# Who adds up the squares of a norm, and where three small steps stand in their queues: a two-layer diffusion backbone on one core

## The reference

```python
x += 1/2 * gate1 * RMSNorm_post(SwiGLU_1(RMSNorm_pre(x) * (1 + scale1) + shift1))
x +=       gate2 * RMSNorm_post(Mixer_l (RMSNorm_pre(x) * (1 + scale2) + shift2))
x += 1/2 * gate3 * RMSNorm_post(SwiGLU_2(RMSNorm_pre(x) * (1 + scale3) + shift3))

def rmsnorm(x, g):
    xf = x.astype(jnp.float32)
    return (xf * lax.rsqrt(jnp.mean(xf * xf, axis=-1, keepdims=True) + EPS) * g).astype(x.dtype)
```

## Time and profile before

| | |
|---|---|
| median of 3 runs | 3075.51 us (3073.78 to 3078.9) |
| profiled execution | 3073.78 us, span 3072.0 us |
| mean granted TensorE clock | 0.976 |
| PE busy | 2852.7 us (93%) |
| DVE, ACT, POOL busy | 1816.0 (59%), 1040.4 (34%), 330.8 (11%) us |
| chain that ended last | PE 77%, DVE 11%, ACT 4%, POOL 3%, issue 3%, DMA 2% |
| costliest line | L1577, PE, 70% of the chain |

### The profile page before, as it was taken

How to read it: one execution, slowest core, us unless ns; L and a number is a source line. 1 busy time by engine, 2 the same in 40 slices (tenths; PEclk the granted TensorE clock), 3 DMA queues, 4 the chain that set the end, 5 groups by cost and what they waited for, 6 DMA issues and landing times.

```text
span 3072.0 us, 47247 instructions
## 1 busy us (share of the span) xinstructions
PE 2852.7 (93%) x19418; PEld 2728.2 (89%) x19418; DVE 1816.0 (59%) x2715; ACT 1040.4 (34%) x1684; POOL 330.8 (11%) x269
## 2 busy tenths in 40 slices
PE   0999999997789999999999999999878898999998
PEld 0999999986579999999999999999844598999997
DVE  7566665755657555657664646457777737532334
ACT  2311114444765211134311125653323424311123
POOL 2000002100021000012000002100027612000002
PEclk9999999999999999999999999999989998999999
DMA  5445544421033443443443433622210133422233
GB/s 190 136 151 173 162 152 139 132 90 44 22 97 116 157 151 126 151 148 107 158 153 126 154 110 119 178 87 71 90 45 28 39 103 103 124 85 68 76 98 115
DMA packets 105174, 351.36 MB, mean 114 GB/s; under 512 B 11008, under 2 KB 27648, under 8 KB 104576
## 3 DMA queue, kind: packets, MB, share of 16 engines
q1 hardware_dynamic: 99328, 339.30, 34.7%
q10 hardware_dynamic: 5632, 9.05, 0.8%
HBM read 337.69 MB, written 10.62 MB: 113 GB/s over the span
## 4 chain that ended last, share of the span: by engine, by line
PE 77%; DVE 11%; ACT 4%; POOL 3%; issue 3%; DMA 2%; DVEq 0%; ACTq 0%; POOLq 0%; SPq 0%
PE P L1577 70%; DVE cv L1467 3%; POOL nbuf L604 2%; DVE wl L1017 1%; ACT pb L807 1%; DVE st L1147 1%; PE P L1499 1%; ACT wh L696 1%; PE P L1745 1%; DMA raw<-wgu_d 1%; PE P L1816 1%; DMA mraw<-wmod_d 1%; POOL mraw L623 1%; PE P L1601 1%; PE P L1518 1%
## 5 line engine op out<-in xcount | busy, mean ns | idle before, releaser
L1577 PE MATMUL P<-xh,wh 128*128 128x320 f32 x4016 | 1021.9, 314 | 5.9 <-DVE xl L1359 4.2
L1577 PE MATMUL P<-xl,wh 128*128 128x320 f32 x4016 | 1010.1, 311 | 0.0
L1577 PE MATMUL P<-xh,wl 128*128 128x320 f32 x4016 | 1009.9, 311 | 0.0
L696 ACT CAST wh<-raw 128x1024 fp32r<-128x1024 f32 (+1 forms) x431 | 481.8, 1118 | 1031.8 <-PE P L1577 840.1
L1017 DVE TENSOR_TENSOR wl<-raw,wh 128x1024 fp32r<-128x1024 f32 (+1 forms) x431 | 574.3, 1333 | 318.5 <-ACT wh L696 318.2
L1577 PEld LDWEIGHTS P<-xh,wh 128*128 128x128 f32 x4016 | 700.5, 189 | 16.0 <-issue 12.5
L1577 PEld LDWEIGHTS P<-xl,wh 128*128 128x128 f32 x4016 | 700.1, 189 | 1.7 <-issue 1.2
L1577 PEld LDWEIGHTS P<-xh,wl 128*128 128x128 f32 x4016 | 699.9, 189 | 0.0
L604 POOL TENSOR_TENSOR nbuf<-nbuf 128x320 f32<-128x320 f32 x144 | 196.4, 1367 | 2340.7 <-ACT nbuf L711 2334.9
L1577 PE MATMUL P<-hh,wh 128*128 128x320 f32 x1408 | 383.5, 313 | 0.0
L1577 PE MATMUL P<-hh,wl 128*128 128x320 f32 x1408 | 380.5, 311 | 0.0
(11 more groups left out here) (228 smaller groups left out, 2400.0 us busy)
## 6 DMA issues: line engine op xcount, KB each, us to landing
raw<-wgu_d SPq DMA_DIRECT2D x216, 512.0 KB, 3.8
mraw<-wmod_d SPq DMA_DIRECT2D x144, 512.0 KB, 3.6
raw<-wdB_d SPq DMA_DIRECT2D x64, 704.0 KB, 4.1
raw<-wdA_d SPq DMA_DIRECT2D x32, 704.0 KB, 5.5
raw<-ain_d SPq DMA_DIRECT2D x28, 512.0 KB, 3.5
raw<-sz_d SPq DMA_DIRECT2D x26, 512.0 KB, 3.9
raw<-sx_d SPq DMA_DIRECT2D x24, 512.0 KB, 3.6
raw<-aout_d SPq DMA_DIRECT2D x16, 512.0 KB, 3.6
```

The lines of the kernel that those rows point to most:

```text
L696: nc.scalar.copy(wh[:, u.u % SPLITS, 0:n], raw[:, u.u % 2, 0:n]).then_inc(hi_done, 1)
L1577: ins = nc.tensor.matmul(P[:, u.banks[i], 0:C], w[:, u.u % SPLITS, k * 128:(k + 1) * 128], m[:, k, C * h:C * h + C], start=(k == 0 and w i ...
```

## The change

Four things, all in the order or the division of work:

1. For PRE norms POOL adds k = 2, 4 and 6 only, and PE takes 1, 3, 5 and 7. Both tables of places change, and the counters with them.
2. `dg` gets three full blocks of 128: DVE writes them with one instruction; PE spreads with two matmuls, of 256 and 64 columns.
3. On DVE, `low` of unit u+2 stands ahead of the windows' work.
4. On ACT, `decays(n)` stands behind the output step of its unit szB n.

```diff
-        ADDED = {PRE: (1, 2, 3, 4, 5, 6), POST: (1, 2, 3, 4, 5, 6)}
-        DIRECT = {PRE: (7,), POST: (7,)}
+        ADDED = {PRE: (2, 4, 6), POST: (1, 2, 3, 4, 5, 6)}
+        DIRECT = {PRE: (1, 3, 5, 7), POST: (7,)}
...
-        PRE_DIRECT = {0: {(3, 9): 7}, 1: {(6, 0): 7}}
+        PRE_DIRECT = {0: {(2, 9): 1, (3, 0): 3, (3, 6): 5, (3, 9): 7}, 1: {(3, 4): 1, (4, 4): 3, (5, 4): 5, (6, 0): 7}}
...
                 elif p.name in ("sz", "szB"):
-                    if p.name == "szB":
-                        decays(u.n)
                     i, n = z_units.index(u), p.w0 + u.n
...
                     act.dma_start(d["zspill"][n][:, c0:c1], zb[:, i % 4, c0:c1]).then_inc(z_out[i % 4], 16)
+                if p.name == "szB":
+                    decays(u.n)
...
-                V.tensor_tensor(dg[:, h, 0:256].rearrange("p (b c) -> p b c", b=2), bc_mid(ident, 2), bc_last(r3[:, h, 1, 0:2], 128), ALU.mult)
-                V.tensor_scalar(dg[:, h, 256:C], ident[:, 64:128], r3[:, h, 1, 2:3], None, ALU.mult).then_inc(dg_done[h], 1)
+                V.tensor_tensor(dg[:, h, :, :], bc_mid(ident, 3), bc_last(r3[:, h, 1, :], 128), ALU.mult).then_inc(dg_done[h], 1)
...
+                if u.u + 2 < len(units):
+                    low(units[u.u + 2])
                 if where == "L1":
                     window0(s, i)
                 if where == "F0" and s:
                     window1(s, i)
                 if where == "F1" and i == 0 and s:
                     lows(s, 1, KD - 2)
                     lows(s, 1, KD - 1)
-                if u.u + 2 < len(units):
-                    low(units[u.u + 2])
...
-                nc.tensor.matmul(scale, ones[:, :], dg[:, h, :], start=True, stop=True).then_inc(rb_ready[h], 1)
+                nc.tensor.matmul(scale[:, 0:256], ones[:, :], dg[:, h, 0:2, :].rearrange("p b c -> p (b c)"), start=True, stop=True)
+                nc.tensor.matmul(scale[:, 256:C], ones[:, :], dg[:, h, 2, 64:128], start=True, stop=True).then_inc(rb_ready[h], 1)
```

More of the change, by code:

```diff
@@ L210, in build @@
         nbuf = sb("nbuf", [128, 6 * C])
-        dg = sb("dg", [128, 2, C])
+        dg = sb("dg", [128, 2, 3, 128])
         mod = sb("mod", [128, 2 * MT, 2])
@@ L479, in norm_total @@
             return P[:, norm_bank(kind, s, h), C:C + 3]
-        ADDED = {PRE: (1, 2, 3, 4, 5, 6), POST: (1, 2, 3, 4, 5, 6)}
-        DIRECT = {PRE: (7,), POST: (7,)}
+        ADDED = {PRE: (2, 4, 6), POST: (1, 2, 3, 4, 5, 6)}
+        DIRECT = {PRE: (1, 3, 5, 7), POST: (7,)}
         def added_before(kind, s):
-            return 12 * s + (6 if kind else 0)
+            return 9 * s + (3 if kind else 0)
         def direct_before(kind, s):
-            return 0
+            return 3 * s + (3 if kind else 0)
         def sq_slot(h, k):
```

## The result

The changed kernel takes 3146.11 us (median of 5 runs, 3144.38 to 3148.43) against 3075.51 (3073.78 to 3079.07): ratio 1.0226, 95% interval 1.0212 to 1.0241, so 70.6 us slower. The prediction had the sign and said 3110, with a range up to 3128. The profiled execution took 3143.89 us, its span is 3142.1.

What follows compares the result with a forecast made beforehand. PE was taken as the bound, with its waits and low clock: 3073.8 - 62.3 (these) + 20.1 (totals) + 7.7 (remaining waits) + 22.3 (`low`) + 2.4 (spread) + 17 (clock) + 29.3 (decays) = 3110.3 us; 8-in-10 range 3090 to 3128.

Steps and rivals of the forecast that it cites:

- the part on `low`: DVE's `low` ahead of the windows: waits for ACT's cast delay the spread at ten places, 22.3 us, bounds 0 and 35.
- everything behind `low` is late: Rival, 3135 us, chance 0.10: updates, squares and totals late, last lows stop PE in F1 unit 0; price 35 us.
- -62.3 + 20.1 + 7.7: Norm boundaries on PE: 62.3 us of waits and clock go, 20.1 of added totals come, 7.7 of waits stay.
- The spread behind `low`: Ten spread places in L1 and F0: new PE waits of 1.8 to 4.5 us each, 22.3 us in all.
- the 17: Low clock at the ten norm places: 1.7 us at each, 17 us, between 0 and 34.
- 2.4 us: Two matmuls for the spread: some 0.11 us more on PE, 22 times, 2.4 us (0 to 5).
- the 2.1 stated: Low clock behind each szB wait for decays: 2.1 us taken, 8.6 us together.
- 29.3 forecast: Decays behind the z output, szB to middle of next unit: 20.7 us of waits plus 8.6 of clock, 29.3.
- the rival on them: Table switches in szB's waits: a drain of 1.38 us per load, 8.3 us more, near 3118, chance 0.01.
- the forecast of +7.2: L1 and F0 windows at five boundaries, parts 1, 2 and the spread behind `low`: +7.2 us predicted.
- faster: Rival, 3060 us, chance 0.05: the cast ends before the root, so the spread isn't late at the ten places.

Runs made afterwards that it cites:

- e1_low: Only `low` of unit u+2 moved ahead of the windows' work on DVE, against the kernel before: 3124.18 us, ratio 1.0151.
- e8_fix: The changed kernel with `low` behind the window again only in F0 units 7 to 9 and F1 unit 0: 3113.73 us, 1.0123 to the kernel before.
- x1_all4: The kernel before with `low` first only in F0 units 7 to 9 and F1 unit 0: 3102.76 us, ratio 1.0083.
- e4_low_back: The changed kernel with part 3 undone (`low` behind the windows again), parts 1, 2 and 4 kept: 3087.6 us, 1.0039 to the kernel before.
- e3_direct: Part 1 alone (PRE totals partly direct on PE) against the kernel before: 3048.14 us, ratio 0.9909.
- b2_totals: Part 1 alone with three of PE's places for totals and spreads later: 3037.78 us, 0.9872 to the kernel before.

## Why the prediction was wrong

- **The step that failed** is in the part on `low`: "So DVE now waits for ACT, and what stands behind is the spread", with a term for the spread's ten places alone. F0 units 7 to 9 and F1 unit 0, where `low` moved as well, stand at nothing without a reason. But `normed` stands behind `low` there, ACT's shift behind `normed`, and ACT's next cast behind the shift. A late step that feeds the next cast is late again one unit on, and what PE asks for is at the end of that row, in F1. The term was 0 and measured 28.2 us (`e1_low`, `e8_fix` and `x1_all4` agree). The rival "everything behind `low` is late" named the place, "the last lows of half 1 stop PE in F1 unit 0", with 0.10. Its 35 us of waits are near what came (17.2 for the spread and 19.2 for `xl`, 36.4), and its 3135 is 11 us short. Its other half, totals that wait longer, did not come: their waits are 7.9 us, and 7.1 with `low` behind the windows (`e4_low_back`). The trace of before showed how little room there was: F1 unit 0 of sub-layer 3 lasts 3.76 us (the start of the next is the second row) where its matmuls need 3.52, since PE already meets the last `lows` as they end.

```profile
1469.33 0.31 PE L1577 MATMUL P<-xh,wh 128*128 128x320 f32 x1
...
1473.09 0.31 PE L1577 MATMUL P<-xh,wh 128*128 128x320 f32 x1
```

- **Part 1** was right in kind. -62.3 + 20.1 + 7.7 is -34.5, plus a part of the clock; alone it measures -28.4. L1498 has the 504 records forecast. What is left of the PRE totals' waits is 7.9 us (5.1 on POOL, 2.8 on ACT) for the 7.7 forecast: 3.3 in the three 11-tile L1 (2.55), 3.9 in the two others (4.8), 0.7 in F0 behind the z output (0.3). The start, put at nothing, is 3.6 us shorter in `e3_direct`.
- **The spread behind `low`** is right in sum and not in detail. `e8_fix` less `e4_low_back` is 26.1 us, for waits of 22.3 and a share of the 17. The ten waits are 17.2 us by the trace. Most in L1 are 1.2 to 1.5, not 2.2, because the unit before the spread runs at the low clock behind the total's wait: PE comes later by itself. Only at the third boundary does the low clock start behind the spread, and there the wait is 2.62; in `e8_fix` it stands ahead of it at that boundary too, and the wait is 1.61. The four plain ones in F0 are 1.4 for 1.8, the one in sub-layer 4 3.4 for 4.5. A wait and the clock behind another wait were added up in the sum, and partly cover each other.
- **Part 2**: 2.4 us were forecast; alone it gives 4.7 back, in `b2_totals` it costs 8. What it does to PE was sized well: on a dense queue the second matmul behind the spread starts 0.80 us after it where it was 0.68, 0.12 more for the 0.11 forecast. What else comes with it is near what a run can tell, and its sign depends on the rest.
- **The clock**: 16.4 us at the norm's places for 17, without the two stretches that stood before, and 10.9 in szB for 8.6 (four times the 2.1 stated are 8.4).
- **Part 4** was right wait by wait: 6.2, 5.6, 5.2, 3.7 forecast, 6.47 (of which 0.21 stood there before), 5.55, 5.22, 3.82 measured; with the clock 29.3 forecast and 31.2 measured (32.5 alone). Six table switches lie in these waits and leave no room for the further 8.3 us that the rival on them (0.01) asked for.
- **Without the missed term** the sum was good: 3110.3 + 28.2 = 3138.5, against 3143.9 of the profiled execution. Part of that is luck: in L1 and F0 the measured waits, totals and clock add up to +2 with the 62.3 taken off, the starts of the units say +6.8, and the forecast of +7.2 meets this with 5 us too much for the spread. What the 5 us between are is open.
- **A slip beside it**: the rival "faster" leaves the 7.7 us of remaining waits out; with them it is 3069, not 3060.

## What to carry to other kernels

When an instruction that waits for another engine is moved ahead of others in a queue, follow the chain out of the place until it comes back to its own queue: if it does, compare the time of one turn with the time of the loop that it feeds (3.8 and 4.6 us against 3.5 here), not the single wait. The delay then appears where the row of turns ends, units later, under the name of the last step. And keep parts apart: of four edits the first gains 28 us by itself, the second 5 at most, and only the third and fourth made the change a loss.

## What the hardware showed that I had not expected

**DVE's diagonals beside POOL's add.** In the changed kernel `dg` takes 0.56 us 19 times and 1.01 us five times (the row at 1412.62 is one), each of the five in L1 while a POOL add of 1.6 to 2.0 us is running, and each ends 0.41 to 0.42 us behind that add's end (1413.63 against 1413.22 here). With `low` behind the window (`e4_low_back`) no add runs beside it and all 24 take 0.56. With `low` first and the two instructions of before (`e1_low`) the first of them is slow at the same five places, 0.88 us. So the new order also put the spread's last step into POOL's time, 0.45 us at five places, and at the third boundary that is what the wait has above the forecast (2.62 for 2.2). A span on POOL is rough in the profile. The Trainium skill (SBUF — State Buffer, "SBUF: two separate sides") says that a DVE operation with two SBUF inputs and a GpSimd operation that reads SBUF share a pair of ports as an exclusive lock, and that the later one fully blocks. By that `dg` would begin when the add ends and take 0.56 us more; the trace has 0.41, near it and a little less.

**The same wait can cost clock or not.** At the same total PE waits 1.0 us in `e3_direct` and in `e4_low_back`. Behind it the clock is at 1.00 in the one and 0.50 in the other, 3.4 us on 6.8 (the total itself, then the stretch behind, of each kernel):

```profile
1871.31 1.50 PE L1499 MATMUL P<-ones,nbuf 128*128 128x1 f32 x12 [1.01 <-POOL nbuf L604]
```
```profile
1871.30:1878.00 6.70, 6.69 (x47) 6.53 (x48) 3.03 (x9) 3.17 (x7) 0.87 (x1) 1.00 0.04 17
```
```profile
1873.17 2.01 PE L1498 MATMUL P<-ones,nbuf 128*128 128x1 f32 x12 [1.00 <-POOL nbuf L604]
```
```profile
1874.00:1880.80 6.80, 6.80 (x26) 6.65 (x27) 1.13 (x3) 2.00 (x3) 0.87 (x1) 0.50 0.01 5
```

So the clock's price of a wait near 1 us is best given as a range (here 0 to 3.4 us a place). Whether the gains of the parts add up can't be read closely from this: by the medians the four parts alone sum to +47 us and are +71 together, by the spans of the traced executions to +66 and +70. How much of the difference is real, and how much of that is clock, isn't shown.
